# Hybrid decoder step on one core: two low-half subtractions moved ahead on VectorE, and the mix product written out on TensorE

## The reference, cut to what matters

```python
merged = jax.nn.sigmoid(gate_a) * (o_attn @ w_pa) + jax.nn.sigmoid(gate_r) * (o_rnn @ w_pr)
x = x + rmsnorm(merged @ w_out, g_mix_post)
f = rmsnorm(x, g_ffn_pre)
g_, u_ = jnp.split(f @ w_gate_up, 2, axis=-1)
x = x + rmsnorm((jax.nn.silu(g_) * u_) @ w_down, g_ffn_post)
```

## Time and profile before

| what | value |
|---|---|
| median of 3 runs | 808.5 us (806.24 to 808.62) |
| the profiled execution, its own time | 807.31 us |
| its span, first to last instruction | 805.5 us |
| mean granted TensorE clock over the span | 0.987 of full |
| PE busy | 777.1 us (96%) |
| DVE busy | 472.3 us (59%) |
| ACT busy | 358.1 us (44%) |

### The profile page before, as it was taken

How to read it: one execution, slowest core, us unless ns; L and a number is a source line. 1 busy time by engine, 2 the same in 40 slices (tenths; PEclk the granted TensorE clock), 3 DMA queues, 4 the chain that set the end, 5 groups by cost and what they waited for, 6 DMA issues and landing times.

```text
span 805.5 us, 16337 instructions
## 1 busy us (share of the span) xinstructions
PE 777.1 (96%) x6019; PEld 736.3 (91%) x6019; DVE 472.3 (59%) x739; ACT 358.1 (44%) x614; POOL 62.4 (8%) x142
## 2 busy tenths in 40 slices
PE   3999999999999999999999899999999999999996
PEld 2879998999898899996889899999999999999996
DVE  5556646636646643675558877777777776222223
ACT  6235534534534541333465455555555565222222
POOL 3321102011010110004000000000000010000000
PEclk9899999999999999999999999999999999999998
DMA  6654335335422122635443233333333224323222
GB/s 205 176 165 134 101 117 142 91 97 146 126 75 83 52 80 72 218 105 167 148 132 104 56 101 105 104 104 104 104 103 96 61 96 135 99 72 91 78 65 111
DMA packets 148746, 89.09 MB, mean 111 GB/s; under 512 B 8594, under 2 KB 142186, under 8 KB 148715
## 3 DMA queue, kind: packets, MB, share of 16 engines
q1 hardware_dynamic: 146014, 81.63, 34.4%
q0 software_dynamic: 2384, 6.40, 2.3%
q10 hardware_dynamic: 316, 0.66, 0.3%
HBM read 81.85 MB, written 6.81 MB: 110 GB/s over the span
## 4 chain that ended last, share of the span: by engine, by line
PE 91%; DVE 1%; ACT 1%; issue 1%; DVEq 0%; ACTq 0%
PE ps L843 32%; PE ps L1158 25%; PE ps L1223 17%; PE ps L1057 6%; PE ps L1127 3%; PE ps L932 1%; PE ps L945 1%; PE ps L962 1%; PE ps L1004 1%; PE ps L907 1%; PE ps L918 1%; PE ps L975 1%; PE ps L1065 0%; PE ps L1092 0%; PE ps L991 0%
## 5 line engine op out<-in xcount | busy, mean ns | idle before, releaser
L1762 DVE TENSOR_TENSOR w_lo<-w_raw,w_hi 128x1024 fp32r<-128x1024 f32 (+1 forms) x68 | 80.9, 1191 | 141.5 <-ACT w_hi L1300 141.2
L1300 ACT ACTIVATE w_hi<-w_raw 128x1024 fp32r<-128x1024 f32 (+1 forms) x68 | 70.0, 1031 | 142.2 <-PE ps L1223 82.6
L843 PE MATMUL ps<-xin_hi,w_hi 128*128 128x272 f32 x576 | 126.9, 302 | 0.0
L843 PE MATMUL ps<-xin_hi,w_lo 128*128 128x272 f32 x576 | 119.5, 289 | 0.0
L843 PE MATMUL ps<-xin_lo,w_hi 128*128 128x272 f32 x576 | 119.4, 289 | 0.0
L843 PEld LDWEIGHTS ps<-xin_hi,w_hi 128*128 128x128 f32 x576 | 90.6, 190 | 8.9 <-issue 7.6
L843 PEld LDWEIGHTS ps<-xin_lo,w_hi 128*128 128x128 f32 x576 | 91.0, 189 | 0.0
L843 PEld LDWEIGHTS ps<-xin_hi,w_lo 128*128 128x128 f32 x576 | 90.6, 190 | 0.0
L1223 PE MATMUL ps<-hid_hi,w_hi 128*128 128x272 f32 x352 | 76.0, 291 | 0.4 <-DVE hid_lo L2140 0.4
L1223 PE MATMUL ps<-hid_lo,w_hi 128*128 128x272 f32 x352 | 75.0, 287 | 0.0
L1223 PE MATMUL ps<-hid_hi,w_lo 128*128 128x272 f32 x352 | 74.9, 288 | 0.0
(11 more groups left out here) (335 smaller groups left out, 1753.5 us busy)
## 6 DMA issues: line engine op xcount, KB each, us to landing
w_raw<-in_w_in_dram SPq DMA_DIRECT2D x72, 256.0 KB, 3.2
g_raw<-in_w_gate_up_dram SPq DMA_DIRECT2D x40, 256.0 KB, 3.9
w_raw<-in_w_down_dram SPq DMA_DIRECT2D x40, 256.0 KB, 2.9
u_raw<-in_w_gate_up_dram SPq DMA_DIRECT2D x20, 256.0 KB, 3.0
e_raw<-in_w_gate_up_dram SPq DMA_DIRECT2D x20, 256.0 KB, 4.4
kc<-in_cache_k_dram SPq DMA_DIRECT2D x64, 64.0 KB, 1.9
vc<-in_cache_v_dram SPq DMA_DIRECT2D x64, 64.0 KB, 2.0
wo_raw<-in_w_out_dram SPq DMA_DIRECT2D x12, 256.0 KB, 4.0
```

The source lines that it names most:

```text
L843: mm = e.matmul(ps[:, bank + h, 0:HT], wt[:, kw, :], xt[:, kx, h * HT:h * HT + HT], start=first and wt is wh and xt is xh, stop=last and ( ...
L1300: e.activation((to or w_hi[s])[:, 0:k, :], w_raw[s][:, 0:k, :], ACT.Copy).then_inc(hi_done, count)
L1762: e.tensor_tensor(wl[:, 0:k, :], w_raw[s][:, 0:k, :], wh[:, 0:k, :].bitcast(F32), ALU.subtract).then_inc(lo_done, count)
```

## The change

On PE, the loop over the mix becomes plain Python, so that its eight tiles stand one after another in PE's instructions; their waits are for constants. The wait for `tile_free[1]` stands between the two halves of the first tile instead of ahead of it.

On DVE, `low_a(1, 1)` and `low_d(0, 0)` stand ahead of `t_low(XT4, ...)` and the three sums of block 1, in that order, instead of behind them.

```diff
-            for s in range(2):
-                e.wait_ge(tile_free[s], 4 * PAIRS + GT_TAIL // 2 + 1)
-            with e.Fori(0, KD // 2) as n:
-                for s in range(2):
-                    split_ready(n * 2 + (C_MIX + s))
-                    e.wait_ge(mix_free, n * 2 + (s + 1))
-                    steps(s, 4 * s, ocat_hi, ocat_lo, [(k, k) for k in range(PAIRS)], True, True)
-                    steps(s, 4 * s + 2, ocat_hi, ocat_lo, [(k, k) for k in range(PAIRS, 2 * PAIRS)], True, True
-                          ).then_inc(tile_done, 1)
+            e.wait_ge(tile_free[0], 4 * PAIRS + GT_TAIL // 2 + 1)
+            for i in range(KD):
+                s = i % 2
+                split_ready(C_MIX + i)
+                e.wait_ge(mix_free, i + 1)
+                steps(s, 4 * s, ocat_hi, ocat_lo, [(k, k) for k in range(PAIRS)], True, True)
+                if i == 0:
+                    e.wait_ge(tile_free[1], 4 * PAIRS + GT_TAIL // 2 + 1)
+                steps(s, 4 * s + 2, ocat_hi, ocat_lo, [(k, k) for k in range(PAIRS, 2 * PAIRS)], True, True
+                      ).then_inc(tile_done, 1)
@@
             low_c(0, 0)
             gate_1(0, 0)
+            low_a(1, 1)
+            low_d(0, 0)
             t_low(XT4, t_raw[:, 2, :, :], 2)
             sum_5(1, 0, 1)
             sum_76(1, 0, 1)
             sum_3(1, 1)
-            low_d(0, 0)
-            low_a(1, 1)
```

## The result

The changed kernel took 802.24 us (median of 4 runs, 801.57 to 802.94) against 808.04 for the kernel before in the same comparison (4 runs, 806.24 to 808.62). The ratio is 0.9938, 95% interval 0.9925 to 0.9951, so 4.0 to 6.1 us less. The forecast was 802.9 in a range of 800.9 to 805.6. The profiled span is 799.8 us where 799.9 had been worked out.

The account below looks back on a forecast made before the run. PE was taken to bound the kernel, so time is won only where it stands still or runs slowly. 1.45 + 2.62 + 1.52 = 5.6 us gained gives 802.9 us from the median of 808.5, range 800.9 to 805.6.

Parts of the forecast that it names:

- The mix's first wait: PE's entrance to the mix: splitting the wait gains 1.45 us, 1.35 of stop and 0.10 of start-up; other bound 0.
- The loop written out: PE's mix loop: removed jumps against 576 more instructions, taken as 0, with a loss of 1.0 us as bound.
- The order on DVE: FFN entrance: PE starts at 449.95 instead of 452.57, 0.04 us behind `t_low`; 2.62 us gained.
- What stands behind it: Following FFN blocks: `low_a(2, 0)` has 0.17 us of slack, DVE catches up within two periods; 0, or 0.3 us lost.
- The clock: Behind the FFN entrance wait: sixteen matmuls at half clock return to full clock, 1.52 us gained; other bound 0.
- Rival 1: FFN entrance: the low clock stays though the wait goes; 4.1 us gained, 804.4 us, chance 0.08.
- rival 2: FFN: PE waits at `t_low` and again for `low_a(2, 0)`, by 1.2 us; 4.4 us gained, 804.1 us, chance 0.12.
- Rivals 3 and 4: 3: FFN gain eaten by later stops, 807.0 us, chance 0.09; 4: instruction fetches at FFN loop jumps, 813.6 us, 0.04.
- The range: Whole kernel: 800.9 to 805.6 us, from the runs' spread of 2.4 us below and rivals 1 and 2 with losses above.

Follow-up runs that it names:

- written_out_only: Kernel before with the mix loop written out, both `tile_free` waits still ahead of it and the old DVE order; 807.51 us, ratio 1.0001.
- mix_only: Kernel before with only the PE half of the change (mix written out, first wait split), old DVE order; 805.82 us, ratio 0.9987.
- stop_for_sum3: Changed kernel, but PE also waits for `sum_3(1)` at the FFN entrance; 806.12 us.
- low_d_behind: Changed kernel, but `low_d(0, 0)` goes back behind the three sums while `low_a(1, 1)` stays ahead; 805.58 us.
- wait_inside: Changed kernel, with PE's wait for `xq_l` moved from ahead of the FFN loop to the first line inside it; 802.14 us.
- stop_for_sum76: Changed kernel, but PE also waits for `sum_76(1)` at the FFN entrance; 805.75 us.

## Why the prediction was right, step by step

- **The mix's first wait, 1.45 us.** Seam 1.35, to the hundredth as worked out; the start-up of 0.10 is part of what the mix segment gained. The middle is unchanged to 0.01 us: the picture did move forward as a piece.
- **The loop written out, 0 (0 to a loss of 1.0).** Right in kind. The mix segment is 0.22 us shorter, of which 0.10 is that start-up. The rest is at tiles 5 and 7, which wait for their `w_lo`: in the changed kernel the chain shows 0.02 us of issue time ahead of each of them. In the kernel before PE restarted 0.13 us behind that low half's end, with the wait one instruction ahead of the matmul; in the changed kernel, where the count is a constant and the wait sits on the matmul, 0.05. This split is good to some 0.05 us: written_out_only keeps the stop, and its mix is still 0.17 us shorter and not 0.12.
- **The order on DVE, 2.62 us.** The mechanism and DVE's times were right, the size was not quite: 2.29. The term "PE starts 0.04 us behind" (0.05 by the rows) was taken from a wait that sits on the matmul, while the new last wait sits four instructions ahead of it, in front of the loop. It cost 0.35.
- **What stands behind it.** The slack for `low_a(2, 0)` came out at 0.25 us for 0.17 worked out. "It catches up within two" periods was wrong: the slack at the next blocks is 0.25, 0.96, 1.53 and 2.24 us, so it takes four. What slows it is a wait that the prediction had not followed: ACT's `snap_7` (L1616, writes `ub`) waits for `hid`, the last in DVE's period, and `up_2`, the first in DVE's next one, waits for `snap_7`. The loads also come into view (DVE waits 0.17 us for `e_raw`). None of this reaches PE.
- **The clock, 1.52 us.** The size was right for this pair of profiles (1.50). The step "I take the whole as gained" was too sure: three profiles of the kernel before show the drop once. What an average execution gains is a part of 1.5 us, and which part these runs don't show. It was luck that the profile the prediction was read from was the one with the drop. The median of the runs hides this, because the timed gain has an uncertainty of about 1 us.
- **Rivals.** Rival 1 as put (the drop has nothing to do with the stop) fell: the two kernels with a stop put back show it again, the six profiles without any stop of over 0.9 us in the FFN don't, and in all fourteen the clock is 1.00 everywhere else from the mix to 790 us. Of rival 2, 0.3 us came true at `t_low` and nothing at `low_a`. Rivals 3 and 4 fell.
- **The range.** It held, but its working was loose: half of the spread of 2.4 us gives 801.7 to 804.1 and not 801.5 to 804.3, and rivals 1 and 2 together (1.5 and 1.2 us) already fill 805.6, so that the losses of 0.3 and of up to 1.0 had no room in it.

That the span came out at 799.8 us for 799.9 owes something to luck: by the segments 5.37 us were won where 5.6 had been worked out, 1.50 of it by a drop that two of three profiles of the kernel before don't have, and a start that happened to be 0.33 us earlier made up for it.

## What to carry to other kernels

When work is put in another order to end a wait, ask of each moved instruction what its count lets go, loads above all: here the smaller of the two moves, which PE did not need yet, was worth 3 us through the loads behind it. A wait belongs on the instruction that needs the data; ahead of a loop, a few instructions earlier, it costs some tenths of a microsecond even when nothing else is late. And where one profile shows a stretch at half clock behind a stop, take several before its price is put down as won.

## What the runs showed of the hardware that I had not expected

- **A stop of the same length doesn't always cost the clock.** Stops of PE in the FFN, with what followed: 2.28 us, drop; 2.61 us, drop in two traces (the kernel before, mix_only) and none in three (written_out_only and the kernel before twice); 3.04 us, drop in stop_for_sum3 and none in low_d_behind, whose clock is 1.00 in the 5 us behind it. No stop of 1.2 us or less brought one from the mix on. Each drop cost 1.5 us. The drop doesn't keep a fixed distance from the restart: in the kernel before PE restarts at 452.57 and the clock falls between 453.8 and 453.9, 1.2 to 1.3 us later; in mix_only, behind a stop of the same 2.61 us, it restarts at 450.83 and the clock falls between 451.2 and 451.3, 0.4 to 0.5 us later. Why one stop brings a drop and another doesn't stays open; the moment at which the stop falls is a candidate, which this agrees with, but these runs were not made to single it out.

Busy time by stretch around the fall, the kernel before and then mix_only:

```profile
452.60:453.80 1.20, 1.20 (x9) 1.20 (x10) 1.20 (x2) 0.00 (x0) 0.00 (x0) 1.00 0.71 211
453.90:457.20 3.30, 3.30 (x17) 3.30 (x16) 1.23 (x2) 0.40 (x1) 0.00 (x0) 0.50 0.87 235
```

```profile
450.80:451.20 0.40, 0.37 (x3) 0.37 (x4) 0.40 (x2) 0.00 (x0) 0.00 (x0) 1.00 0.26 74
451.30:451.80 0.50, 0.50 (x5) 0.50 (x4) 0.50 (x1) 0.00 (x0) 0.00 (x0) 0.50 0.91 264
```

The stop of 3.04 us without a drop, low_d_behind:

```profile
461.13 0.36 PE L1159 MATMUL ps<-xq_hi,c_hi 128*128 128x272 f32 x1 [3.04 <-ACT xsnap L1621]
```

```profile
461.00:466.00 5.00, 4.84 (x36) 4.66 (x37) 3.97 (x6) 2.43 (x4) 0.00 (x0) 1.00 0.58 164
```

By the rule of the Trainium skill that the prediction weighed (page "TensorE: Matmul & The Clock Gate", section "Why this matters for your kernels"), gaps of 2.28 and 2.61 us keep the clock, while one of 3.04 lies right at its bound. The traces here don't bear the rule out: three contradict it (2.28 us once, 2.61 twice) and three agree (2.61 each); the two of 3.04, one with a drop and one without, speak neither way.

- **Where a wait sits on PE sets the restart.** The time from the end of the instruction waited for to the start of PE's first matmul, by how far ahead of this matmul the instruction that carries the wait stands in PE's list (from the unrounded traces, so 0.01 us off the rows in places):

| ahead of the matmul by | restart, us | where |
|---|---|---|
| 0, the matmul itself | 0.05 | `a_lo` in the kernel before; `w_lo` of mix tiles 5 and 7 in the changed one |
| 1 | 0.13 | `w_lo` of the same two tiles in the kernel before |
| 2 | 0.24 | `xq_lo` in wait_inside |
| 3 | 0.39 | `gates` in written_out_only |
| 4 | 0.35 | `xq_lo` in the changed kernel |
| 5 | 0.44, 0.46, 0.49 | `gates` in the kernel before; stop_for_sum76; stop_for_sum3 |

The two rows for `gates` are released by ACT, the others by DVE. The instructions in between are of several kinds (a branch, counts in registers, waits already met); what each kind costs was not taken apart.
